# A router in whole tiles, shared-expert products split in four, and weight loads issued earlier, in a two-layer mixture-of-experts kernel

## The reference

```python
scores = sigmoid(xf @ w_router);  biased = scores + router_bias
gmask  = 4 best of 8 groups (sum of the two best in each)
_, eidx = top_k(where(gmask, biased, -inf), 8)          # 8 of 64 experts
wts    = take(scores, eidx) / sum * 2.5
# each expert: swiglu(rows, w_gate[e], w_up[e]) @ w_down[e], D_EXPERT = 256
out    = sum over the 8 experts of wts * expert(xf) + swiglu(xf, shared weights)
```

## Time and profile before

| what | value |
|---|---|
| runs | 2644.52, 2645.62, 2645.91 us |
| the profiled execution: its own time | 2642.83 us |
| its span on the core | 2640.6 us |
| busy | PE 2402.9, DVE 785.4, ACT 570.4, POOL 146.3 us |
| moved by DMA | 599.72 MB, mean 227 GB/s |
| chain that ended last | PE 82%, DMA 7%, DVE 5%, issue 3%, ACT 2% |
| router of layer 0, from the first score to the first gate/up product of an expert | 809.8 to 905.2 us |
| router and shared expert of layer 1 | 2057.8 to 2123.2 us |
| experts | 905 to 1461 us and 2123 to 2622 us |

### The profile page before, as it was taken

How to read it: one execution, slowest core, us unless ns; L and a number is a source line. 1 busy time by engine, 2 the same in 40 slices (tenths; PEclk the granted TensorE clock), 3 DMA queues, 4 the chain that set the end, 5 groups by cost and what they waited for, 6 DMA issues and landing times.

```text
span 2640.6 us, 41238 instructions
## 1 busy us (share of the span) xinstructions
PE 2402.9 (91%) x17286; PEld 1365.7 (52%) x17286; DVE 785.4 (30%) x1929; ACT 570.4 (22%) x1132; POOL 146.3 (6%) x154
## 2 busy tenths in 40 slices
PE   7999988999998898999998799988999799967997
PEld 3466477644445443333333556767788644433444
DVE  1364455311114431111111525555411521111112
ACT  3455223300002011111111144433210111100111
POOL 0000000000000111111111000000000011100100
PEclk9999999999997799999999899999999699988999
DMA  7101142411102699999999631122331599999993
GB/s 321 71 10 41 37 157 103 188 64 64 64 0 110 243 422 420 413 406 424 403 408 393 260 146 67 70 70 94 143 147 64 204 393 423 419 408 417 413 423 163
DMA packets 67640, 599.72 MB, mean 227 GB/s; under 512 B 13182, under 2 KB 13310, under 8 KB 25600
## 3 DMA queue, kind: packets, MB, share of 16 engines
q1 hardware_dynamic: 50032, 555.09, 51.9%
q0 software_dynamic: 17424, 41.99, 4.2%
HBM read 588.63 MB, written 26.75 MB: 233 GB/s over the span
## 4 chain that ended last, share of the span: by engine, by line
PE 82%; DMA 7%; DVE 5%; issue 3%; ACT 2%; another core or an unknown queue 0%; SPq 0%; ACTq 0%; DVEq 0%
PE bank L1870 10%; PE bank L1345 9%; PE bank L2296 7%; PE bank L292 6%; PE bank L1885 5%; PE bank L2310 3%; PE bank L1360 3%; PE bank L1350 3%; PE bank L2316 3%; PE bank L384 3%; DMA ring<-in_wexp 2%; DMA arena<-in_wexp 2%; PE bank L1034 2%; PE bank L1049 2%; PE bank L309 1%
## 5 line engine op out<-in xcount | busy, mean ns | idle before, releaser
L1870 PE MATMUL bank<-ring,arena 128*32 128x512 f32 (+2 forms) x1248 | 297.5, 610 | 16.5 <-issue 15.2
L1345 PE MATMUL bank<-normed,ring 128*128 128x512 f32 (+1 forms) x768 | 255.5, 486 | 0.0
L2296 PE MATMUL bank<-ring,arena 128*32 128x512 f32 (+2 forms) x832 | 193.4, 621 | 18.1 <-issue 16.6
L1345 PEld LDWEIGHTS bank<-normed,ring 128*128 128x128 f32 x768 | 145.9, 190 | 101.8 <-issue 91.8
L1870 PEld LDWEIGHTS bank<-ring,arena 128*32 128x32 f32 (+2 forms) x1248 | 94.7, 131 | 154.0 <-issue 152.0
L292 PE MATMUL bank<-normed,ring 128*128 128x512 f32 (+1 forms) x416 | 160.5, 544 | 0.0
L1870 PE MATMUL bank<-branches,arena 128*32 128x512 f32 (+2 forms) x400 | 134.3, 594 | 6.3 <-issue 6.3
L1885 PE MATMUL bank<-arena 128*32 128x512 f32 (+2 forms) x384 | 112.8, 596 | 7.0 <-DMA arena<-in_wexp 3.3
L292 PEld LDWEIGHTS bank<-normed,ring 128*128 128x128 f32 x416 | 78.4, 190 | 77.8 <-issue 75.3
L2060 DVE TENSOR_TENSOR arena<-bank,arena 128x256 f32<-128x256 f32 x43 | 18.3, 425 | 324.0 <-ACT arena L1979 324.0
L2296 PE MATMUL bank<-normed,arena 128*32 128x512 f32 (+1 forms) x256 | 92.9, 644 | 21.0 <-issue 18.1
(11 more groups left out here) (484 smaller groups left out, 3828.5 us busy)
## 6 DMA issues: line engine op xcount, KB each, us to landing
ring<-in_wexp SPq DMA_DIRECT2D x87, 2048.0 KB, 14.5
ring<-in_wst SPq DMA_DIRECT2D x54, 2048.0 KB, 8.4
arena<-in_wexp SPq DMA_DIRECT2D x70, 1024.0 KB, 20.4
branches<-in_wexp SPq DMA_DIRECT2D x31, 2048.0 KB, 13.8
ring<-in_wexp SPq DMA_DIRECT2D x60, 1024.0 KB, 12.1
normed<-in_wexp SPq DMA_DIRECT2D x12, 2048.0 KB
arena<-expert_rows SPq DMA_DIRECT2D x6, 2048.0 KB, 11.0
branches<-expert_rows SPq DMA_DIRECT2D x2, 2048.0 KB, 14.4
```

Source lines behind the costliest of these rows:

```text
L1345: last = nc.tensor.matmul(ps[2 * (n % 4)][:, c0:], wg[:, k, i * P:(i + 1) * P], H[:, k, c0:], start=(k == 0), stop=(k == KD - 1))
L1870: last = nc.tensor.matmul(ps[2 + s][r0:r1, :], XT_[:, s, k * P + r0:k * P + r1], wt[:, k, :], start=(k == 0), stop=(k == KD - 1))
L2296: last = nc.tensor.matmul(ps[5][r0:r1, :], XT_[:, s, k * P + r0:k * P + r1], w[:, k, :], start=(k == 0), stop=(k == KD - 1))
```

## The change

1. An extra Ln of one column stands in front of the norm's wait for TensorE.
2. The slots of a tile's eight choices come from one `max` over slots times selection; the two one-hots of a tile are made by one instruction each for all eight choices; ScalarE multiplies by the choice's number, eight instructions a tile; the buffers hold two tiles.
3. `shared_gate_up` is split into four quarters. Gate of m = 0 stands ahead of the wait for the selection, up of m = 0 and gate of m = 1 ahead of the one-hot products, up of m = 1 behind them. The positions are made in pieces, behind the rows per expert, and have a signal of their own.
4. The shared weights are issued ahead of the writes of `hidden_rows` in layer 0, the first six loads of layer 1 too. In layer 1 the fifth expert's loads go ahead of the wait for the shared down product, which itself moves behind unit 0's gate/up product. TensorE waits later for the shared hidden values.
5. Layer 1's smalls and its first two chunks are issued right behind the combine's blocks; the wait for `sh["res"]` stands in front of the third.

```diff
         def norm_act_rs(act, ch, l, w, c0):
+            ch.link(nc.scalar.activation(arena(4640, 1), cn("eps", 1), ACT.Ln))
             act.wait_ge(norm["mm"], nth(w, l) * NORM["mm"] + 1)
...
+            shared_gate_up(pe, l, 0, 0)
             pe.wait_ge(ro["sel"], l * RO["sel"] + 1)
-            for t in range(t0, TT):
-                for u in range(t0, t + 1):
-                    nc.tensor.matmul(ps[2]... positions of all tiles
             (rows per expert: L1448, L1450) ... .then_inc(ro["pos"], 1)
+            for t in range(t0, TT - 2):
+                positions(t)
             pe.wait_ge(ro["rk"], l * RO["rk"] + 1)      # L1454
+            positions(TT - 2)
             pe.wait_ge(ro["rk"], l * RO["rk"] + 2)      # L1456
-            shared_gate_up(pe, l, 0)
+            positions(TT - 1).then_inc(ro["pos"], 1)
+            shared_gate_up(pe, l, 0, 1)
+            shared_gate_up(pe, l, 1, 0)
             for i, (t, k) in enumerate(chosen):
-                pe.wait_ge(ro["hot"], l * RO["hot"] + i + 1)
+                pe.wait_ge(ro["hc"], l * RO["hc"] + 2 * (TT - t0) + i + 1)
...
-            shared_gate_up(pe, l, 1)
+            shared_gate_up(pe, l, 1, 1)
...                                                      # ro_act
+            for n, t in enumerate(range(t0, TT)):
+                act.wait_ge(ro["hot"], l * RO["hot"] + n + 1)
+                for k in range(HOT):
+                    part = r_val[:, n % 2, k, 0:PLAN[l].n]
+                    nc.scalar.activation(part, part, ACT.Copy, scale=cn("choice", 1, n * TOPK + k)).then_inc(ro["hc"], 1)
...                                                      # ro_dve
-            for i, (t, k) in enumerate(chosen):          (32 or 16 reads, L1591)
+            ch.link(V.tensor_tensor(r_keyed[:, t0:, :], r_at[:, t0:, :], r_sel[:, t0:, :], ALU.mult))
+            for t in range(t0, TT):
+                ch.add(V.max(r_dk[:, t, :], r_keyed[:, t, :]))
...
-            for i, (t, k) in enumerate(chosen):          (32 or 16 pairs, L1601, L1603)
+            for n, t in enumerate(range(t0, TT)):
+                if n >= 2:
+                    dve.wait_ge(ro["hotm"], l * RO["hotm"] + (n - 1) * HOT)
+                ch.link(V.tensor_tensor(r_hot[:, n % 2, :, :], bcast(cn("count", P), 1, HOT), bcast(r_p[:, t, :], 2, P), ALU.is_equal))
+                V.tensor_tensor(r_val[:, n % 2, :, 0:at.n], bcast(cn("count", at.n), 1, HOT), bcast(r_u[:, t, :], 2, at.n), ALU.is_equal).then_inc(ro["hot"], 1)
...                                                      # ex_sync, behind gate_up(3, 3, ...)
+            fifth = sp.value_load(EJI[0:1, 4:5], min_val=0, max_val=E)
+            gate_up(fifth, 4, gu5_in[4][0])
             sp.wait_ge(sh["hid"], l * SHN["hid"] + 4)
             down(3, 3, dn5_in[3][0])
+            sp.wait_ge(ro["dk"], l * RO["dk"] + 1)
+            down(fifth, 4, dn5_in[4][0])
             sp.wait_ge(sh["gu"], shared_down_done)
             down(0, 0, dn5_in[0][0])
...                                                      # ex_pe, unit loop
                 if u >= 2:
                     to_tokens(u - 2)
+                elif u == 0:
+                    shared_down()
...                                                      # block.sync
             for l in range(L):
-                if l:
-                    sp.wait_ge(sh["res"], l * SHN["res"])
                 for n, (m, j) in enumerate(ORDER_OF_USE[l]):
+                    if l and n == 2:
+                        sp.wait_ge(sh["res"], l * SHN["res"])
```

More of the change, by code:

```diff
@@ L1407, in build @@
         r_msk, r_rep = arena(4608, TT, E), arena(4864, TT, E)
-        r_pos, r_over, r_at, r_blk = (arena(5120 + 256 * i, TT, E) for i in range(4))
+        r_over, r_at, r_blk = (arena(5120 + 256 * i, TT, E) for i in range(3))
         r_j, r_h, r_spill = (arena(6144 + 256 * i, TT, E) for i in range(3))
@@ L1451, in ro_pe, with positions @@
             last.then_inc(ro["pos"], 1)
+            def positions(t):
+                for u in range(t0, t + 1):
+                    last = nc.tensor.matmul(ps[2][:, t * E:(t + 1) * E], cn("before", P) if u == t else ones, r_sel[:, u, :],
+                                            start=(u == t0), stop=(u == t))
+                return last
+            for t in range(t0, TT - 2):
+                positions(t)
             pe.wait_ge(ro["rk"], l * RO["rk"] + 1)
             nc.tensor.matmul(ps[1][:, E:2 * E], ones[0:E, :], r_beats[0:E, :], start=True, stop=True).then_inc(ro["ranked"], 1)
+            positions(TT - 2)
             pe.wait_ge(ro["rk"], l * RO["rk"] + 2)
@@ L1568, in ro_dve @@
             dve.wait_ge(ro["sel"], l * RO["sel"] + 1)
[L1569 to L1572, removed]
             for s in range(2):
@@ L1587, in ro_dve @@
             place_rows(dve, ch, l, t0)
[L1589 to L1593, removed]
+            ch.link(V.tensor_tensor(r_keyed[:, t0:, :], r_at[:, t0:, :], r_sel[:, t0:, :], ALU.mult))
+            for t in range(t0, TT):
+                ch.add(V.max(r_dk[:, t, :], r_keyed[:, t, :]))
+            ch.settle()
             ch.link(V.tensor_scalar(r_u[:, t0:, :], r_dk[:, t0:, :], 1.0 / P, 0.5 / P - 0.5, ALU.mult, ALU.add))
@@ L1717, in shared_gate_up @@
             w = GU_W[3].rearrange("p (k m) -> p k m", k=KD)
-            for up in range(2):
-                for k in range(KD):
-                    last = nc.tensor.matmul(ps[4 + 2 * up + m][:, c0:], w[:, k, up * FE + m * P:up * FE + (m + 1) * P], H[:, k, c0:],
-                                            start=(k == 0), stop=(k == KD - 1))
-            last.then_inc(sh["gu"], 1)
+            for k in range(KD):
+                last = nc.tensor.matmul(ps[4 + 2 * up + m][:, c0:], w[:, k, up * FE + m * P:up * FE + (m + 1) * P], H[:, k, c0:],
+                                        start=(k == 0), stop=(k == KD - 1))
+            if up:
+                last.then_inc(sh["gu"], 1)
         def px_sync(sp, l, before):
             tiles, at = tiles_of(l), PLAN[l]
+            sp.wait_ge(mg["o"], l * MG["o"] + KD)
+            sp.dma_start(GU_W[3], wexp[l, E, :, 0:GU_N]).then_inc(sh["w"], 16)
             for n, t in enumerate(tiles):
@@ L2049, in add_to_residual, with shared_hidden @@
                 return last
-            for m in range(2):
+            def shared_hidden(m):
                 dve.wait_ge(sh["sig"], l * SHN["sig"] + m + 1)
@@ L2149, in ex_sync @@
             l, at = LAST, PLAN[LAST]
-            for n in range(NX):
-                sp.wait_ge(ro["hc"], l * RO["hc"] + 2 * n + 2)
-                sp.dma_start(hx[l][n * P:(n + 1) * P, :], HTB[:, n, :]).then_inc(ro[f"hs{n}"], 16)
             def gate_up(e, w, done):
@@ L2166, in ex_sync @@
             gate_up(2, 2, gu5_in[2][0])
+            for n in range(NX):
+                sp.wait_ge(ro["hc"], l * RO["hc"] + 2 * n + 2)
+                sp.dma_start(hx[l][n * P:(n + 1) * P, :], HTB[:, n, :]).then_inc(ro[f"hs{n}"], 16)
             sp.wait_ge(ro["end"], l * RO["end"] + 1)
@@ L2275, in ex_pe @@
             freed_by = at.last_use[E - 2 - 4]
-            pe.wait_ge(sh["hid"], l * SHN["hid"] + 4)
-            pe.wait_ge(*shared_down_in)
-            wt = DN5[0].rearrange("p (k m) -> p k m", k=2)
-            for m in range(KD):
-                for k in range(2):
-                    last = nc.tensor.matmul(acc(m), wt[:, k, m * P:(m + 1) * P], SH[:, k * T + TC:(k + 1) * T], start=(m % 2 == 0 and k == 0), stop=False)
-            last.then_inc(sh["gu"], 1)
+            pe.wait_ge(sh["hid"], l * SHN["hid"] + 2)
             def flip_rows(s, half, freed=None):
@@ L2354, in to_tokens, with shared_down @@
                 combine(u % 2).then_inc(un["pe"], 1)
+            def shared_down():
+                pe.wait_ge(*shared_down_in)
+                wt = DN5[0].rearrange("p (k m) -> p k m", k=2)
+                for m in range(KD):
+                    for k in range(2):
+                        last = nc.tensor.matmul(acc(m), wt[:, k, m * P:(m + 1) * P], SH[:, k * T + TC:(k + 1) * T], start=(m % 2 == 0 and k == 0), stop=False)
+                last.then_inc(sh["gu"], 1)
             flip_left(0)
             flip_right(0)
+            pe.wait_ge(sh["hid"], l * SHN["hid"] + 4)
             for u in range(U):
```

50 lines of the change are left out of this document (20 added, 30 removed).

## The result

The changed kernel takes 2613.11 us (median of 4, 2610.12 to 2618.89) against 2645.76 (2644.52 to 2652.57) for the kernel before on the same chip: ratio 0.9874, 95% interval 0.9849 to 0.9899. A second set of runs gave 2615.96 against 2646.02, ratio 0.9886 (0.9870 to 0.9903). So 30 to 33 us are gained, where 21.3 were forecast; 2624.3 was predicted, 2612 to 2636 the range.

The account below looks back on a forecast made before the run. Routers were taken as bound by chains of small steps, experts by the weight stream, the boundary by SP's wait for the residual. Router 0 -15.1, layer 1 -6, boundary -0.4, table +0.2: -21.3 from 2645.62 gives 2624.3 us, range 2612 to 2636.

Parts of the forecast that it names:

- the forecast's own case: Whole kernel: the summed gain of 21.3 us gives 2624.3 us, running from 2617 to 2631; chance 0.66.
- more is gained: Routers and experts: TensorE's lead passes whole, 20 + 10 us, with the clock staying up; 2617 us, chance 0.13.
- Leading quarter and counts: Layer 0's router: first quarter ends at 840.5, rows per expert at 841.9, 1.3 us later than before; slots at 855.3.
- One-hots: Layer 0's router: wide VectorE passes take 1.23 and 0.80 us a tile; TensorE, not VectorE, is late.
- the rival with 4.4 us a tile: Chosen stage: broadcast one-hots cost VectorE as much as before, so only 7 + 4 us are won; 2634, chance 0.07.
- Chosen products: Layer 0's router: tiles 2 and 3 take 3.6 us each at low clock, ending at 875.9 instead of 881.48.
- Last quarter: Layer 0's router: ends at 888.8 instead of 901.15, first gate/up at 890.1 instead of 905.24; router gains 15.1 us.
- Layer 1's router: Same edits on two tiles: leading quarter costs 0, unit 0's gate/up starts at about 2106.4 instead of 2123.20.
- Stream: Layer 1's weight loads: the fifth expert's go out ahead of expert 0's down, gaining 6 us (bounds 2 to 10).
- Boundary: Between layers 0 and 1: chunks land earlier, but ScalarE's modulation ends the first accumulation, leaving a gain of 0.4 us.
- Table: Norms: Ln's table load already runs ahead of the wait for TensorE; the added instruction costs 0.2 us (0 to 0.5).
- given back: Experts: only loads released by the last quarter move, and units waiting for landings return the rest; 2637 us, chance 0.08.

Follow-up runs that it names:

- load-order kernel: Changed kernel with layer 1's fifth-expert loads back behind expert 0's down, as before; layer 1's end came 5.9 to 6.6 us later, router unchanged at 50.0.
- kernel with late chunks: Changed kernel with layer 1's first ring chunks sent only once layer 0's whole residual is written, as before; boundary stretch 87.7 us, time unchanged.

## Why the prediction came out as it did

The mechanisms were right in the main, and the gain was 1.4 to 1.5 times the forecast's. The time lies only 1.1 us above the lower end of the range, and below the 2617 to 2631 of the forecast's own case: it was the width given to the rival "more is gained" that held it, so that it is inside is in part luck. The mis-sized term is, in both routers, the time of TensorE's small products and of the quarters beside them, priced for a low clock. The steps, on the axis of the kernel before:

- **Leading quarter and counts.** Ends 840.5 (forecast 840.5), counts 841.9 (841.9), slots 855.7 (855.3), two quarters 864.3 (864.7). Right.
- **One-hots.** VectorE's wide passes took 1.22 and 0.79 us (1.23 and 0.80 from the earlier trace rows). Right; the rival with 4.4 us a tile is out. That 32 pairs in the new order cost router 0 3.7 us more shows the trade. The Trainium skill's faster tier of tensor_scalar ("VectorE: DVE Perf Modes", "The perf-mode tier table") speaks for the pairs, and that run is against it.
- **Chosen products: mis-sized.** I priced tiles 2 and 3 at 3.6 us each, for a clock that falls once the large products end. It stayed at 1.00, and they took 4.2 us together: end 872.8, not 875.9.
- **Last quarter.** 8.8 us (9.5), first gate/up 885.9 (890.1). Router 0 gained 19.2 instead of 15.1 in the first pair of profiles, 18.6 from two each.
- **Layer 1's router: mis-sized the same way.** The leading quarter was put at 0; it held the clock, and the two quarters end 2085.8 (2089.7): they start 2.8 us sooner than forecast and take 8.5 (9.53). The chosen products take 4.0 us (5.4) and end 2090.6 (2095.1), first gate/up 2100.8 (2106.4). In between, TensorE waits 0.80 us for VectorE and ScalarE, which I had not foreseen: here their chain is the path.
- **Stream.** Expert 0's down was forecast to go out 1.7 us later than before, and went out 4.5 earlier. With the 7.5 us of the fifth expert ahead of it that makes 12.0; 10.4 was measured, 6 forecast. The load-order kernel shows the 7.5 as about 6.3.
- **Boundary.** 0.4 forecast; the run with the old wait shows nothing that can be told from spread. The sign for it came as forecast: TensorE waits for ScalarE there, not for a load. **Table.** +0.2 as forecast: at 2602.37 the load, at 2603.67 the added instruction, at 2603.90 Ln.

The rival "more is gained" had half of the cause: the clock stayed up. Its 20 + 10 us came nearer than my sum (18.6 and 10.4 measured; 30 would be 2615.6, it was carried as 28 and 2617). That the lead passed whole held in layer 0, whose experts lost nothing of it, but not in layer 1: its router gained 22.4 us, its second unit began 16.3 us sooner (2102.70; 9.6 forecast), and its end came 10.1 sooner. The 9 us of the rival "given back" don't follow from its own terms either; 12 halved and 2 make 8. One of my tests was badly put. An expert stage in layer 1 more than 3 us longer than 499 was to speak against the forecast, yet my own sum (first gate/up 16.8 earlier, end 6 earlier) made it 10.8 longer; it became 12.3 longer. Another sign against me did appear, in small: VectorE was not to release TensorE in the chosen stage. In layer 0 it stands in that chain once, for tile 2, with 0.75 us of TensorE's wait behind it (ended by ScalarE), and in layer 1 ahead of the first tile, with 0.80: stops, not a pace.

## What to carry to other kernels

Price small products at the clock that the stretch will have after the change, not the one it had: the chosen stage was slow both because VectorE paced it and because that pace went with a low clock, and one edit removed both (17.8 us became 8.6 in the kernel with that edit alone). Where a stream of loads sets the time of a stage, follow the instruction that feeds its queue next; here first products 5 to 7 us later cost nothing, and that instruction 9 us sooner gave 3 to 4. Work put into an idle gap in front of a chain on the path is worth its length less what it sticks out of the gap, and before moving work that releases loads, see which small transfer would then stand behind them.

## What was not expected of the hardware

- The leading quarter of layer 0 took 8.7 or 8.8 us in five profiles and 7.1 in five others, with the same code up to there. The window over it had a granted clock of 1.00 in the kernel with late chunks (825 to 832) and 0.81 in the changed kernel's second profile (832 to 841). Router 0 is 86.3 or 87.8 us accordingly; what made the level rise earlier is open.
- The shortest landing of layer 1's gathers was 8.3 us instead of 4.0 when two 2 MB loads had been sent 5 to 6 us ahead of the first one.
- Untouched stages of 780 and 535 us vary by 12 us between executions, more than most single edits here are worth. In the second the range lies in one stretch, 148 us at a granted clock of 0.98 and 158 at 0.92. Only cutting the traces at the same instructions made edits of 3 to 6 us readable.
